# Dilated attention with both heads of a pair in one pipeline unit over half of the keys

## What is computed

```python
DIL_PATTERNS = ((128, 1), (512, 4), (2048, 16))
def dilated_attention(q, k, v):
    outs, lses = [], []
    for w, r in DIL_PATTERNS:      # keys at distances 0, r, 2r, ..., w
        o, lse = banded_attn(split(q)[:, :, None], split(k), split(v), w // r)
        ...
    wts = jax.nn.softmax(jnp.stack(lses, axis=0), axis=0)
    return jnp.sum(wts[..., None] * jnp.stack(outs, axis=0), axis=0)
```

## Time and profile before

| | us |
|---|---|
| median of 3 runs | 2419.43 (2416.67 to 2425.9) |
| the profiled execution | 2421.15 |
| its span, from the first instruction to the last | 2419.4 |
| PE busy | 2359.7 |
| DVE, POOL, ACT busy | 1459.7, 1103.5, 834.6 |

### The profile page before, as it was taken

The page is one execution under the profiler, slowest core; times in us unless marked ns, Lnnn a source line. Parts: engine busy times, 40 slices in busy tenths (PEclk is TensorE's granted clock), DMA queues, the critical chain, the costliest instruction groups (busy, mean ns, idle before and its releaser), DMA issues.

```text
span 2419.4 us, 34453 instructions
## 1 busy us (share of the span) xinstructions
PE 2359.7 (98%) x12184; PEld 1986.7 (82%) x12184; DVE 1459.7 (60%) x2846; ACT 834.6 (34%) x1717; POOL 1103.5 (46%) x994
## 2 busy tenths in 40 slices
PE   6999999998999999999999999999999999999999
PEld 5787878787987888888888788888988888888887
DVE  6464655546157766675684566663366776667674
ACT  5424343332132322232232555553232232223230
POOL 5223131312236745574573733432255674557461
PEclk9999999999999999999999999999999999999999
DMA  4011010103121021102111300012022102210201
GB/s 137 14 27 27 27 27 20 34 7 103 44 70 53 18 69 61 60 17 69 61 40 53 109 24 24 27 36 92 27 70 70 53 17 69 67 54 17 87 28 77
DMA packets 140981, 120.35 MB, mean 50 GB/s; under 512 B 26048, under 2 KB 126912, under 8 KB 140864
## 3 DMA queue, kind: packets, MB, share of 16 engines
q1 hardware_dynamic: 133488, 103.70, 13.9%
q10 hardware_dynamic: 7376, 15.12, 1.8%
HBM read 110.41 MB, written 8.39 MB: 49 GB/s over the span
## 4 chain that ended last, share of the span: by engine, by line
PE 83%; DVE 9%; POOL 3%; issue 2%; ACT 2%; DMA 1%; SPq 0%; DVEq 0%; ACTq 0%; POOLq 0%
PE gp L463 13%; PE gp L465 12%; PE gp L464 12%; PE sc L465 6%; PE sc L463 6%; PE sc L464 6%; PE o_ps L564 4%; PE sc L530 3%; PE tp L464 2%; PE tp L463 2%; PE tp L465 2%; PE tp L552 2%; PE sc L535 1%; PE qt L465 1%; PE qt L463 1%
## 5 line engine op out<-in xcount | busy, mean ns | idle before, releaser
L463 PE MATMUL gp<-W_hi,hT_hi 128*128 128x384 f32 (+1 forms) x1152 | 421.6, 366 | 5.9 <-POOL W_lo L1740 5.5
L465 PE MATMUL gp<-W_hi,hT_lo 128*128 128x384 f32 (+1 forms) x1152 | 383.5, 333 | 0.0
L464 PE MATMUL gp<-W_lo,hT_hi 128*128 128x384 f32 (+1 forms) x1152 | 382.7, 332 | 0.0
L1865 POOL TENSOR_TENSOR W_lo<-af,W_hi 128x512 fp32r<-128x512 f32 x168 | 239.5, 1425 | 282.5 <-ACT W_hi L1045 282.5
L1845 POOL TENSOR_TENSOR W_lo<-raw,W_hi 128x1024 fp32r<-128x1024 f32 x72 | 187.4, 2608 | 230.0 <-ACT W_hi L987 217.2
L1559 DVE TENSOR_TENSOR af<-af 128x512 f32<-128x512 f32 x112 | 81.2, 725 | 300.5 <-ACT af L1028 300.5
L1865 POOL TENSOR_TENSOR W_lo<-rb,W_hi 128x512 fp32r<-128x512 f32 x168 | 245.8, 1463 | 0.0
L463 PEld LDWEIGHTS gp<-W_hi,hT_hi 128*128 128x128 f32 x1152 | 220.1, 191 | 15.6 <-issue 5.7
L464 PEld LDWEIGHTS gp<-W_lo,hT_hi 128*128 128x128 f32 x1152 | 220.4, 191 | 0.0
L465 PEld LDWEIGHTS gp<-W_hi,hT_lo 128*128 128x128 f32 x1152 | 218.8, 190 | 0.0
L463 PE MATMUL gp<-hT_hi,W_hi 128*128 128x512 f32 x512 | 199.5, 390 | 0.0
(11 more groups left out here) (294 smaller groups left out, 5259.4 us busy)
## 6 DMA issues: line engine op xcount, KB each, us to landing
raw<-in_mlp_w_up SPq DMA_DIRECT2D x64, 512.0 KB, 4.2
rb<-in_mlp_w_down SPq DMA_DIRECT2D x56, 512.0 KB, 5.4
raw<-in_hyb_w_in SPq DMA_DIRECT2D x74, 128.0 KB, 2.3
X<-in_x SPq DMA_DIRECT2D x8, 512.0 KB, 7.3
X<-in_x ACTq DMA_DIRECT2D x8, 512.0 KB, 3.5
raw<-in_mlp_w_down SPq DMA_DIRECT2D x8, 512.0 KB, 3.2
raw<-in_swa_w_qkv SPq DMA_DIRECT2D x16, 256.0 KB, 3.1
x_spill<-X ACTq DMA_DIRECT2D x8, 512.0 KB, 2.7
```

Source lines behind the costliest of these rows:

```text
L463: mm(o, a[0], b[0], start=first, stop=False)
L464: mm(o, a[0], b[1], start=False, stop=False)
L465: return mm(o, a[1], b[0], start=False, stop=last)
L1865: E.tensor_tensor(WF_lo[:, c], x(k), WF_hi[:, c].bitcast(f32), ALU.subtract).then_inc(op_ready, 1)
```

## The change

The pipeline unit of the dilated attention becomes a part: both heads of the pair for query block a, over the first 512 keys (c = 0) or, for blocks 4 to 7 alone, over the remaining (a - 3) x 128 keys (c = 1). A pair has U_D = 12 parts where it had 16 units. The scores of the two heads of a part follow each other, on the two halves of the rows of PE, into the two banks of sc; so do the copies and outputs of both heads. Part (a, 0) has its scores in the first half of slot a + 2, (a, 1) in the second half. DVE takes a minimum for each head and part, and for blocks 4 to 7 the joint one of the two parts (`max_ready`); ACT takes the exponentials of both heads over all keys of the block at once, after them. The transposes of a part are a slot after its scores and stand ahead of the next part's scores; its values are half a slot after its transposes. On DVE the output of blocks 0 to 3 is the first work of slot a + 4, that of blocks 4 to 7 comes after the retention's rotation. The sliding-window functions lose their `kind` and keep their work; its counts of o_evac and p_ready change with the number of units.

```diff
@@ -83,7 +83,8 @@
     F_O1 = F_S + NG * 32 * KQ
     F_M1 = F_O1 + 32 * (KQ + 2)
 
-    U_S, A_S = NG * 2 * T, NG * T
+    U_D = T + T // 2
+    U_S, A_S = NG * U_D, NG * T
...
@@ -261,9 +263,25 @@
 
             return Pm[:, 0, 0:4 * HD] if kind == "D" and t == 0 and a0 > 0 else sq[:, 0:(4 if kind == "D" else 5) * HD]
 
-        def width(kind, a):
-
-            return (a + 1) * P if kind == "D" else min(a + 1, 2) * P
+        def width(a):
+
+            return min(a + 1, 2) * P
+
+        def part(g, a, c):
+
+            return g * U_D + (a if a < 4 else 2 * a - 4 + c)
+
+        def part_width(a, c):
+
+            return min((a + 1) * P - 512 * c, 512)
+
+        def in_part(a, c):
+
+            return 0 <= a < T and (c == 0 or a >= 4)
+
+        def two_heads(x, w):
+
+            return x.rearrange("p (h n) -> p h n", h=2)[:, :, 0:w]
 
 
...
 
-            def scores(kind, n, u0):
+            def part_scores(g, a, c):
+                pe.wait_ge(qkt_ready, g * T + a + 1)
+                if part(g, a, c) >= 1:
+                    pe.wait_ge(sm_ready, part(g, a, c))
+                if a == 0:
+
+                    pe.wait_ge(ht_ready, T)
+                    if g > 0:
+                        pe.wait_ge(r_x, g * T)
+                w = part_width(a, c)
+                for h in range(2):
+                    r = slice(HD * h, HD * (h + 1))
+                    last = mm(sc[:, h * 512:h * 512 + w], qT[r, a % 2, 0:P], kT[r, c * 512:c * 512 + w], start=True, stop=True)
+                last.then_inc(s_done, 1)
+
+            def part_trans(g, a, c):
+                pe.wait_ge(p_ready, g * T + a + 1)
+                if part(g, a, c) >= 1:
+                    pe.wait_ge(pt_ready, part(g, a, c))
+                for h in range(2):
+                    for x in range(0, part_width(a, c), P):
+                        last = nc.tensor.transpose(tp[:, h * 512 + x:h * 512 + x + P],
+                                                   Pm[:, h, c * 512 + x:c * 512 + x + P], ident[:, :])
+                last.then_inc(tp_done, 1)
+
+            def part_values(g, a, c):
+                pe.wait_ge(pt_ready, part(g, a, c) + 1)
+                pe.wait_ge(v_ready, g * T + a + 1)
+                if c == 0 and g * T + a >= 1:
+                    pe.wait_ge(o_evac, g * T + a)
+                for h in range(2):
+                    for x in range(0, part_width(a, c), P):
+                        b = c * 4 + x // P
+                        last = mm(o_ps[:, h * HD:(h + 1) * HD], pT[:, c, h * 512 + x:h * 512 + x + P],
+                                  V[:, b, h * HD:(h + 1) * HD], start=b == h == 0, stop=b == a and h == 1)
+                last.then_inc(pv_done, 1)
+
...
                         if s < 2:
                             first_T(s, 2 * j + 1)
                         for g, t in now:
-                            n, r = 2 * t + j - 4, t - T - 1
-                            if 0 <= n < 2 * T:
-                                scores("D", n, g * 2 * T)
-                            if 0 <= n - 1 < 2 * T:
-                                trans("D", n - 1, g * 2 * T)
+                            r = t - T - 1
+                            if in_part(t - 3, j):
+                                part_trans(g, t - 3, j)
+                            if in_part(t - 2, j):
+                                part_scores(g, t - 2, j)
                             if j == 0 and 0 <= r - 1 < T:
                                 ret_values(r - 1, g * T + r - 1)
                         next(steps)
                         for g, t in now:
-                            n = 2 * t + j - 4
-                            if 0 <= n - 2 < 2 * T:
-                                values("D", n - 2, g * 2 * T)
+                            if in_part(t - 4 + j, 1 - j):
+                                part_values(g, t - 4 + j, 1 - j)
                         next(steps)
                         if s < 2:
...
                 act.wait_ge(r_qt, n + 1)
                 A(rqT[:, :, :].rearrange("p m c -> p (m c)"), qt[0:HD, 0:3 * P], ACT.Copy).then_inc(r_qtev, 1)
 
-            def probs_T(kind, n, u0):
+            def part_probs_T(g, a, c):
+                w = part_width(a, c)
+                act.wait_ge(tp_done, part(g, a, c) + 1)
+                if in_part(a - 1, c):
+                    act.wait_ge(pv_done, part(g, a - 1, c) + 1)
+                elif g > 0:
+                    act.wait_ge(pv_done, g * U_D)
+                A(two_heads(pT[:, c, :], w), two_heads(tp[:, :], w), ACT.Copy).then_inc(pt_ready, 1)
+
+            def heads_probs(g, a):
+                w = (a + 1) * P
+                if a < 4:
+                    act.wait_ge(sm_ready, part(g, a, 0) + 1)
+                else:
+                    act.wait_ge(max_ready, g * 4 + a - 3)
+                for h in range(2):
+                    z = slice(2 * (a % 4) + h, 2 * (a % 4) + h + 1)
+                    last = A(Pm[:, h, 0:w], Pm[:, h, 0:w], ACT.Exp, scale=-1.0, bias=negm[:, z], accum_out=den[:, z])
...
                                 head_squares("D", t, n0, a0)
                             if j == 1 and 0 <= r < T:
                                 ret_T_copy(r, g * T + r)
-                            n = 2 * t + j - 4
-                            if 0 <= n - 1 < 2 * T:
-                                probs_T("D", n - 1, u0)
-                            if 0 <= n < 2 * T:
-                                probs("D", n, u0)
+                            if in_part(t - 3, j):
+                                part_probs_T(g, t - 3, j)
+                            if in_part(t - 2, j) and j == (t - 2 >= 4):
+                                heads_probs(g, t - 2)
                             if j == 0 and t < 2 * T and t % T in SPLIT_AT:
                                 p = SPLIT_AT[t % T]
...
 
-            def maxima(kind, n, u0, g):
+            def part_maxima(g, a, c):
+
+                k = part(g, a, c)
+                if in_part(a - 1, c):
+                    dve.wait_ge(tp_done, part(g, a - 1, c) + 1)
+                elif g > 0:
+                    dve.wait_ge(tp_done, g * U_D)
+                dve.wait_ge(s_done, k + 1)
+                alone(dve)
+                w, m = part_width(a, c), (T - 1 - a) * P + 512 * c
+                for h in range(2):
+                    z = slice(2 * (a % 4) + h, 2 * (a % 4) + h + 1)
+                    last = E.tensor_tensor_reduce(out=Pm[:, h, c * 512:c * 512 + w], in0=sc[:, h * 512:h * 512 + w],
+                                                  in1=nlm[:, m:m + w], scale=1.0, scalar=3e38, op0=ALU.add, op1=ALU.min,
+                                                  accum_out=(negr if c else negm)[:, z])
+                    if h == 0:
+                        step.did(last)
+                last.then_inc(sm_ready, 1)
+                if c == 1:
+                    z = slice(2 * (a % 4), 2 * (a % 4) + 2)
+                    step.wait()
+                    dve.wait_ge(sm_ready, k + 1)
+                    E.tensor_tensor(negm[:, z], negm[:, z], negr[:, z], ALU.min).then_inc(max_ready, 1)
+
+            def heads_outputs(g, a):
+                z = slice(2 * (a % 4), 2 * (a % 4) + 2)
+                dve.wait_ge(pv_done, part(g, a, a >= 4) + 1)
+                step.did(E.reciprocal(rden[:, z], den[:, z]))
+                step.wait()
+                E.tensor_tensor(X[:, a, bass.ds(g * 2 * HD + D // 2, 2 * HD)].rearrange("p (e d) -> p e d", e=2),
+                                o_ps[:, 0:2 * HD].rearrange("p (e d) -> p e d", e=2),
+                                rden[:, z].rearrange("p (e o) -> p e o", o=1).to_broadcast([P, 2, HD]), ALU.mult).then_inc(o_evac, 1)
+
+            def maxima(n):
...
                         decays()
                     for j in range(2):
                         for g, t in reversed(live(s)):
-                            n0, u0, a0, r, n = N_DR + g * 2 * T, g * 2 * T, g * T, t - T - 1, 2 * t + j - 4
-                            if 0 <= n - 3 < 2 * T:
-                                outputs("D", n - 3, u0, g)
+                            n0, a0, r = N_DR + g * 2 * T, g * T, t - T - 1
+                            if j == 0 and 0 <= t - 4 < 4:
+                                heads_outputs(g, t - 4)
                             if j == 0 and 0 <= t - 1 < T:
                                 sums("D", t - 1, a0)
                             if s == 1:
@@ -1471,12 +1540,14 @@
                                     dve.wait_ge(act_step, 1)
                                 for i in ((3, 4), (5, 6, 7))[j]:
                                     lo_T(i, 0, 0)
-                            if 0 <= n < 2 * T:
-                                maxima("D", n, u0, g)
+                            if in_part(t - 2, j):
+                                part_maxima(g, t - 2, j)
                             if j == 0 and 0 <= t - 1 < T:
                                 prep("D", t - 1, a0)
```

(44 more changed lines are left out.)

62 lines of the change are left out of this document (25 added, 37 removed).

## The result

The changed kernel takes 2379.73 us in the median of four runs (2376.05 to 2382.43), the kernel before 2421.29 in the median of its four: a ratio of 0.9827, with a 95% interval from 0.9802 to 0.9853. So the medians are 41.6 us apart, and the interval means 35.6 to 47.9 us. The profiled execution took 2382.43 us, 38.7 less than that of before. The forecast was 2381, 38 us less than before, in a range from 2369 to 2401.

A forecast was written before the change was run, and what follows sets the result against it. TensorE, busy 98% of the span, was taken as the bound. Saved 35.4 (scores) + 9 (waits gone) - 4 (slot 9) - 2.4 (slot 2) = 38 us: 2383 against the profiled execution, 2381 on the median's scale; range 2369 to 2401.

The forecast's parts named there:

- Scores: Dilated-attention score blocks on TensorE: two heads cost what one costs, 33.8 us saved, with 16 entries of 0.10 us 35.4 us.
- Rival A: Score parts 512 keys wide (or all) run in three steps of passes, not two: 15 us less won, 2396 us; chance 0.11.
- the rule that the prediction set against the row of 256 keys: TensorE matmuls start and end strictly in program order: two heads over 256 keys would take 0.84 us; the row has 0.64.
- D: Rival: the two heads' score matmuls don't overlap, so scores save only 4.8 us: 2412 us; chance 0.04.
- Waits that go: Values' wait on TensorE for VectorE's evacuation, in slots 3 and 10 of a pair, disappears: 2.2 us a pair, 9 us.
- (1): Transposes wait for both heads' joint exponentials, dearest at block 7: cover 0.4 us, costed at 0, 8 us allowed for the range.
- Rival B: Late chains: exponentials and VectorE's minima 1.5 us late for each of 16 blocks 4 to 7: 2405 us; chance 0.10.
- C: Rival, slower: part transposes wait on joint exponentials without cover, about 3.3 us a block: 53 us lost, 2434 us; chance 0.03.
- (2): In slot 9 the retention's first transpose waits for VectorE's rotation, queued behind minima: 1.0 us a pair, 4 us lost.
- (3): In slot 2 VectorE's rotation of the heads sets the slot's end, so 0.6 us of scores isn't gained: 2.4 us in four pairs.
- Slot 3, where I feared the same: GpSimd's subtraction might collide with VectorE's rotation of the heads: no loss expected, up to 1.8 us a pair, 7 in all.

The follow-up runs named there:

- the heads apart: Changed kernel, but in 10 of 12 parts a pair head 0's scores come ahead of the transposes and head 1's behind them: 2422.73 us, ratio 0.9988.
- The two delays: Changed kernel with four, then eight, tiny chained copies on ScalarE ahead of the joint exponentials of blocks 4 to 7: 2381.25 and 2395.81 us, one run each.
- the shifted split: Changed kernel with the split of the next weights (ScalarE, then GpSimd) one slot later, in slots 3 to 6 and 11 to 14: 2378.12 us, ratio 0.9808.

## Why the prediction was right, by its steps

**Scores.** Read from start to next, all score blocks of the stage took 74.7 us before and take 40.6 now, 34.1 less; the forecast had 33.8, from lines through the same rows. That two heads cost what one costs holds at 128, 256, 384 and 512 keys (0.42, 0.63, 0.85, 1.06 us). With the heads apart it is all lost (two parts of a pair keep them together there, and they keep their 0.42 us). The entries to a score block cost 0.09 us, whether a projection or a transpose is ahead, against 0.10.

**Rival A**, three steps of passes for two heads, is refuted by the 1.06 us above: three steps would have taken 1.48. Its sign was a second head that starts 0.43 us after the first. A timeline of 0.1 us from just before the scores of block 3, first of the changed kernel, then of the kernel with the heads apart, shows how many of their instructions have started:

```profile
189.02 0.70 PE L545 MATMUL sc<-kT,qT 64*128 64x512 f32 x2
```

```profile
202.13 0.69 PE L545 MATMUL sc<-kT,qT 64*128 64x512 f32 x1
```

With both heads two instructions start at once (7 ns apart in the trace), and the other two together 0.53 us later. One head alone starts one, and its second 0.53 us later. So a step contains one instruction of each head. The rows don't name the head, nor the order in which the four were issued. If the instructions of the two heads are issued in turn, none overtakes another; so the rule that the prediction set against the row of 256 keys is not shown to be broken. What is refuted is my working from it, the third step.

**D** is what the kernel with the heads apart is made into, and it came out at 0.9988; my 2412 for it was too low. Without the overlap 48 parts are 96 blocks of one head (88 in that kernel), against 64 before, and I had counted 16 fewer than before.

**Waits that go.** The wait for the evacuation is gone, as forecast. It was worth 2.6 us a pair, not 2.2 (1.28, 0.40 and 0.96 us from start to start, less the usual 0.17), since the modelled ends of the matmuls hide a part of each wait. One wait that I had left as it was shrank too: slots 12 to 14 of the retention are 0.8 us shorter in sum (6.67, 6.95, 6.88 against 6.35, 6.47, 6.88). By the table slot 11 now contains values of block 7 and is 1.8 us longer for TensorE, which may be what gives VectorE its lead; no run here took this apart.

**Waits that come.** (1) None at the joint exponentials. The slack before the transposes was 1.43, 0.93, 0.45 and 0.74 us for blocks 4 to 7, where I had counted over 1, over 1, and 0.4 for the last two. I had the wrong block as the dearest: behind block 7 stands the retention's work, behind block 6 does not. The two delays show that this slack is all there is. Rival B, 1.5 us late in each block, would so have cost 2.7 us a pair (1.5 and the 0.07 of hand-over less each slack), not the 6 I gave it, and C, decided at 2.4 us a block by my count, only beyond 3 us. (2) Slot 9: 0.93 us a pair, forecast 1.0. (3) Slot 2: 1.55 us idle where it was 0.91, forecast 0.6 more. That is three pairs and not four: in the first L1452 runs free. Slot 3, where I feared the same, is free. That the subtraction is the cause in slot 2, and worth more than what was lost to it, the shifted split shows.

**The sum.** A pair was to give 9.5 us (38 in four) and gave 10.6 in the second and third, and 10.0 from the start of the fourth to the end of the stage. From the first projection to the end of the stage the traces give 583.7 and 539.1 us, 44.6 less, of which the first pair has 13.4: its opening slots wait for the start of the kernel and differ between executions (slots 0 to 2 took 33.4 us in the trace of before, and from 28.2 to 31.8 in those of the changed kernel and its variants). Against it, the first projection starts 2.9 us later in the trace of after, and behind the stage 3.1 us are given back, of which the next section tells. 44.6 - 2.9 - 3.1 gives the 38.7 us of the profiled runs. The main term and the mechanism were right, but that the total came within 2 us was in part luck: 0.4 and 0.8 us a pair too little on waits, nothing for the first pair's opening, and nothing for the 6 us lost before and behind the stage, and these misses nearly cancel.

## What to carry to other kernels

Where two matmuls each use half of the rows of TensorE, put them directly next to each other: what gains is the adjacency, since the same instructions with a transpose group between them took twice as long. Price it by a place in the trace that already does so, from start to start. Then look for the step of another engine that the shortened stage no longer covers, and for whole-instruction collisions of VectorE and GpSimd; where such work is moved, look up in every slot what it will fall on, as shifting the split by one slot took back in slot 15 (0.57 us) a third of what it gave in slot 2 (1.62 us).

## What the runs showed of the hardware that was not expected

The granted clock fell to the 1.2 GHz level for 3.5 us behind the stage, in the trace of the changed kernel: the stretch before the first block behind the stage (the third of the output projection; two are projected in the last slots), that block's first half, and its end.

```profile
554.00:556.93 2.93, 0.82 (x8) 0.85 (x9) 1.69 (x2) 0.71 (x1) 0.00 (x0) 1.00 0.56 179
556.93:560.46 3.53, 3.53 (x15) 3.53 (x14) 1.23 (x1) 2.50 (x3) 1.40 (x1) 0.52 0.63 216
560.46:562.75 2.29, 2.29 (x15) 2.29 (x15) 0.00 (x0) 0.00 (x0) 2.24 (x2) 0.99 0.64 178
```

TensorE had been idle for 2.5 us just before, waiting for hT_lo. The kernel before has the same idle time at this place, and there the block ran at 1.00:

```profile
598.70:602.95 4.25, 4.25 (x27) 4.25 (x26) 1.23 (x1) 2.51 (x3) 2.11 (x2) 1.00 0.68 240
```

It cost 1.6 us (5.82 and 4.25). Of the eight experiments, three had the block in 4.25 to 4.27 us and five in 4.9 to 5.8, with the same instructions. In four of these five the last slot of the stage is longer too (10.05 to 10.20 us, not 9.43), so the low clock began there; both together cost 1.4 to 1.6 us in each of the five. So it differs between executions, and no run here shows what decides it. The other 1.5 us behind the stage are 0.4 in the first MLP and 1.1 in the sliding-window stage, where TensorE waited 3.4 us for the rotation of the heads instead of 2.1 and 1.2 for kT instead of 0.2. The clock also fell at different places of that stage: in the trace of before it was 0.50 from 1371.4 to 1374.8 us, 14 us into the stage, in that of after 1.00 at the same place (1331.5 to 1334.9). The change doesn't touch the work there, and whether this belongs to it or to the execution stays open.
